# Expert-weight matrices in batches of eight tokens, built by VectorE and ScalarE alone

## The reference

```
e = (jnp.take_along_axis(i1, ci // PEER_TOPK, axis=-1) * N_KEYS
     + jnp.take_along_axis(i2, ci % PEER_TOPK, axis=-1))
g = jax.nn.softmax(sc.astype(jnp.float32), axis=-1).astype(h.dtype)
...
act = jnp.einsum('td,tkd->tk', xt, u_tab[et])
return jnp.einsum('tk,tkd->td', jax.nn.gelu(act, approximate=False) * gt, v_tab[et])
```

## Time and profile before

| | us |
|---|---|
| median of three runs | 1732.82 (1732.2 to 1737.53) |
| profiled execution | 1729.81 |
| its span, first to last instruction | 1728.0 |
| PE busy in it | 1652.7 (96%) |
| DVE busy | 1554.6 (90%) |
| ACT busy | 865.5 (50%) |
| POOL busy | 652.7 (38%) |

### The profile page before, as it was taken

One profiled execution on the slowest core, in us unless ns is written; L12 is line 12 of the kernel. 1 busy time (PEld: TensorE's weight loads), 2 busy tenths in 40 slices (PEclk: granted clock), 3 DMA queues, 4 the chain that ended last, 5 costly groups with the idle time before them and its releaser, 6 DMA issues.

```text
span 1728.0 us, 29685 instructions
## 1 busy us (share of the span) xinstructions
PE 1652.7 (96%) x9219; PEld 1387.0 (80%) x9219; DVE 1554.6 (90%) x3206; ACT 865.5 (50%) x2431; POOL 652.7 (38%) x644
## 2 busy tenths in 40 slices
PE   6999889999947999999999999999999999999997
PEld 4566658866636888889999998999999999999996
DVE  3887864499999999999999999999999999999998
ACT  3122573337788994444444444444444444444444
POOL 0000000044458983444444444344444444443442
PEclk9999999999978999999999999999999999999999
DMA  9343102111136779999999999999999999999996
GB/s 359 135 146 112 72 4 97 63 60 51 49 122 208 209 222 356 400 393 402 410 398 395 409 397 396 407 405 398 403 406 394 407 407 394 395 412 406 401 401 211
DMA packets 129315, 505.90 MB, mean 293 GB/s; under 512 B 9184, under 2 KB 64096, under 8 KB 79968
## 3 DMA queue, kind: packets, MB, share of 16 engines
q0 software_dynamic: 36864, 268.45, 38.5%
q1 hardware_dynamic: 92096, 236.49, 36.8%
q10 hardware_dynamic: 288, 0.13, 0.0%
HBM read 477.18 MB, written 25.10 MB: 291 GB/s over the span
## 4 chain that ended last, share of the span: by engine, by line
PE 78%; DVE 15%; issue 3%; ACT 2%; DMA 1%; POOL 0%; SPq 0%; DVEq 0%; POOLq 0%; ACTq 0%
PE psum L851 30%; PE psum L865 30%; PE psum L501 7%; DVE slab L1700 5%; PE psum L739 3%; DVE slab L1704 2%; PE psum L502 2%; DVE slab L1555 1%; DMA slab<-wblk 1%; PE psum L489 1%; DVE slab L1557 1%; PE psum L754 1%; DVE slab L1571 1%; ACT slab L1099 1%; DVE slab L1550 1%
## 5 line engine op out<-in xcount | busy, mean ns | idle before, releaser
L1881 POOL DMA_INDIRECT slab<-table,ixr x256 | 421.0, 1644 | 603.1 <-DVE slab L1750 552.1
L851 PE MATMUL psum<-hhi,uhi 128*128 128x384 f32 x1008 | 339.0, 336 | 1.4 <-issue 1.3
L851 PE MATMUL psum<-hhi,ulo 128*128 128x384 f32 x1008 | 338.4, 336 | 0.0
L851 PE MATMUL psum<-hlo,uhi 128*128 128x384 f32 x1008 | 337.7, 335 | 0.0
L1750 DVE SCALAR_TENSOR_TENSOR slab<-slab,cf 128x1024 f32<-128x1024 f32 x252 | 323.2, 1283 | 14.5
L1740 DVE SCALAR_TENSOR_TENSOR slab<-slab,h2tok 128x1024 f32<-128x1024 f32 x256 | 312.1, 1219 | 25.7 <-DMA slab<-table,ixr 25.4
L865 PE MATMUL psum<-vhi,whi 128*128 128x512 f32 x762 | 297.8, 391 | 3.1 <-DVE wlo L1723 3.1
L865 PE MATMUL psum<-vhi,wlo 128*128 128x512 f32 x762 | 300.1, 394 | 0.0
L865 PE MATMUL psum<-vlo,whi 128*128 128x512 f32 x762 | 299.8, 393 | 0.0
L501 PE MATMUL psum<-slab 128*128 128x512 f32 x464 | 239.1, 597 | 1.9 <-ACT slab L1021 1.1
L1206 ACT CAST whi<-slab 128x384 fp32r<-128x384 f32 x127 | 65.3, 515 | 304.3 <-DVE slab L1735 304.3
(11 more groups left out here) (240 smaller groups left out, 2771.7 us busy)
## 6 DMA issues: line engine op xcount, KB each, us to landing
slab<-ublk SPq DMA_DIRECT2D x64, 1024.0 KB, 9.0
slab<-vtab SPq DMA_DIRECT2D x63, 1024.0 KB, 8.9
slab<-wblk SPq DMA_DIRECT2D x90, 512.0 KB, 4.5
g_dram<-slab SPq DMA_DIRECT2D x11, 1984.0 KB, 8.8
slab<-g_dram SPq DMA_DIRECT2D x31, 704.0 KB, 8.9
slab<-table,ixr POOLq DMA_INDIRECT x256, 10.0
slab<-slab SPq DMA_DIRECT2D x42, 64.0 KB, 10.9
x<-x_in SPq DMA_DIRECT2D x1, 2560.0 KB, 9.2
```

What stands on the lines that cost most here:

```text
L851: last = pe.matmul(psum[:, b, 0:ND], w[:, c, :], m[:, c, :], start=(m_ == 0), stop=(m_ == 3 * DC - 1))
L1881: pool.indirect_dma_start(out=rows[:, sl % GR, :], out_offset=None, in_=table, in_offset=bass.IndirectOffsetOnAxis(ap=ixr[:, half, half_co ...
```

## The change

G is built in batches of eight tokens (`BATCH`, 48 batches), and POOL takes no part. For a batch DVE compares the second halves of eight tokens with 0 to 127 in one bf16 tensor_tensor into `same`, which has the token as its innermost index (L1691 in the new kernel). The table `iota8`, each number eight times, is made once, ahead of the search; `e2b` holds the second halves in bf16. A second tensor_tensor writes all eight rows of `hot_a` (L1695). A third multiplies four tokens of `same` by their weights and writes four rows of `hot_b` through a transposed view (L1698). ACT writes the other four rows of `hot_b` by four scaled copies out of `same`, each reading one token, that is every eighth bf16 (L1152). There are two buffers of `same`, `hot_a` and `hot_b`, eight tokens each. PE does the same matmuls as before; the first four of a batch wait for `hot_a` and ACT's rows, the second four for DVE's rows; in steps 0, 1 and 3 it also waits until ACT has read the bank's earlier contents. POOL issues its first four row fetches together.

```
@@ -141,7 +141,9 @@
-FETCH_AT = (2, 3, 4, 5)
+BATCH = 8
+NB = ND // BATCH
+OWN = BATCH // 2
...
@@ -205,7 +207,9 @@
-        e1T, e2T, gT = (sb(n, [P, ND]) for n in ("e1T", "e2T", "gT"))
+        iota8 = sb("iota8", [P, KEYS, BATCH], BF16)
+        e2b = sb("e2b", [P, ND], BF16)
+        e1T, gT = (sb(n, [P, ND]) for n in ("e1T", "gT"))
...
@@ -262,9 +266,9 @@
-        gnT, away = view(38016, ND), view(256, 4, KEYS)
+        same = [view(c0, KEYS * BATCH // 2).bitcast(BF16).rearrange("p (k t) -> p k t", t=BATCH) for c0 in (256, 37248)]
...
-        hot_a, hot_b = view(9216, 4, 4, P), view(3072, 4, 4, P)
+        hot_a, hot_b = view(9216, 2, BATCH, P), view(3072, 2, BATCH, P)
...
@@ -326,15 +330,9 @@
-        def token_of(b):
-
-            return g_group(b * 4 // TG) * TG + b * 4 % TG
-
-        def hot_a_split(b):
-
-            if b in FETCH_AT:
-                return 0
-            return 1 if b % 4 == 3 else 2
+        def first_token(n):
+
+            return g_group(n * BATCH // TG) * TG + n * BATCH % TG
...
@@ -821,13 +819,18 @@
-                pe.wait_ge(hot_a_set, sum(hot_a_split(n) > 0 for n in range(b + 1)))
-                pe.wait_ge(hot_b_set, b + 1)
-                pe.wait_ge(hot_c_set, b + 1)
+                at, half = divmod(b, 2)
+                if half:
+                    pe.wait_ge(hot_d_set, at + 1)
+                else:
+                    pe.wait_ge(hot_a_set, at + 1)
+                    pe.wait_ge(hot_c_set, at + 1)
                 if b >= 4:
                     pe.wait_ge(g_laid, b - 3)
+                elif b + 4 in SLOT_BANK:
+                    pe.wait_ge(slot_set, SLOT_BANK.index(b + 4) + 1)
                 for m in range(4):
-                    last = pe.matmul(psum[:, 4 + b % 4, m * P:(m + 1) * P], hot_a[:, b % 4, m, :], hot_b[:, b % 4, m, :], start=True, stop=True)
+                    last = pe.matmul(psum[:, 4 + b % 4, m * P:(m + 1) * P], hot_a[:, at % 2, 4 * half + m, :], hot_b[:, at % 2, 4 * half + m, :], start=True, stop=True)
...
@@ -1137,24 +1140,17 @@
-                act.copy(gT[:, t * P:(t + 1) * P], psum[:, SLOT_BANK[k], P:2 * P])
-                act.activation(gnT[:, t * P:(t + 1) * P], psum[:, SLOT_BANK[k], P:2 * P], ACT.Copy, scale=-1.0).then_inc(slot_set, 1)
-
-            def distance(b):
...
-                act.activation(away[:, b % 4, :], con[:, C_IOTA:C_IOTA + KEYS], ACT.Abs, bias=e2T[:, col:col + 1], scale=-1.0).then_inc(away_set, 1)
-
-            def hot_row(b):
...
-                act.activation(hot_b[:, b % 4, 3, :], away[:, b % 4, :], ACT.Relu, bias=gT[:, col:col + 1], scale=gnT[:, col:col + 1])\
-                    .then_inc(hot_c_set, 1)
+                act.copy(gT[:, t * P:(t + 1) * P], psum[:, SLOT_BANK[k], P:2 * P]).then_inc(slot_set, 1)
+
+            def hot_rows(n):
+
+                col, b = first_token(n), n % 2
+                act.wait_ge(same_set, n + 1)
+                if n >= 2:
+                    act.wait_ge(g_made, 2 * n - 2)
+                for m in range(OWN):
+                    last = act.activation(hot_b[:, b, m, :], same[b][:, :, m], ACT.Copy, scale=gT[:, col + m:col + m + 1])
+                last.then_inc(hot_c_set, 1)
...
@@ -1169,15 +1165,11 @@
-            for b in range(3):
-                distance(b)
-            for b in range(2):
-                hot_row(b)
+            hot_rows(0)
             for b in range(ND // 4):
-                if b + 3 < ND // 4:
-                    distance(b + 3)
-                if b + 2 < ND // 4:
-                    hot_row(b + 2)
+                at, half = divmod(b, 2)
+                if not half and at + 1 < NB:
+                    hot_rows(at + 1)
...
@@ -1617,6 +1609,7 @@
+            step(v.tensor_copy(iota8[:], con[:, C_IOTA:C_IOTA + KEYS].unsqueeze(2).broadcast_to([P, KEYS, BATCH])))
             v.tensor_copy(count, con[:, C_AT:C_AT + CAND].unsqueeze(2).broadcast_to([P, CAND, EARLY])).then_inc(topk_step, 1)
...
-                step(v.tensor_copy(e2T[:, part], e2u[:]))
+                step(v.tensor_copy(e2b[:, part], e2u[:]))
...
@@ -1690,30 +1683,35 @@
+            def hot_batch(n):
+                col, b = first_token(n), n % 2
+                if n >= 2:
+                    v.wait_ge(hot_c_set, n - 1)
+                    v.wait_ge(hot_d_set, n - 1)
+                v.tensor_tensor(same[b], iota8[:], e2b[:, col:col + BATCH].unsqueeze(1).broadcast_to([P, KEYS, BATCH]), ALU.is_equal).then_inc(same_set, 1)
+                if n >= 2:
+                    v.wait_ge(g_made, 2 * n - 2)
+                wide = [P, BATCH, KEYS]
+                v.tensor_tensor(hot_a[:, b], con[:, C_IOTA:C_IOTA + KEYS].unsqueeze(1).broadcast_to(wide),
+                                e1T[:, col:col + BATCH].unsqueeze(2).broadcast_to(wide), ALU.is_equal).then_inc(hot_a_set, 1)
+                v.wait_ge(same_set, n + 1)
+                v.tensor_tensor(hot_b[:, b, OWN:].rearrange("p t k -> p k t"), same[b][:, :, OWN:],
+                                gT[:, col + OWN:col + BATCH].unsqueeze(1).broadcast_to([P, KEYS, BATCH - OWN]), ALU.mult).then_inc(hot_d_set, 1)
+
             for k in range(N_DENSE):
                 v.wait_ge(slot_set, k + 1)
-                for b in range(k * P // 4, (k + 1) * P // 4):
-                    if b >= 4:
-                        v.wait_ge(g_made, b - 3)
-                    for m in range(3):
-                        col = token_of(b) + m
-                        v.tensor_scalar(hot_b[:, b % 4, m, :], con[:, C_IOTA:C_IOTA + KEYS], e2T[:, col:col + 1], gT[:, col:col + 1],
-                                        ALU.is_equal, ALU.mult)
-                    m0 = hot_a_split(b)
-                    col, wide = token_of(b) + m0, [P, 4 - m0, KEYS]
-                    v.tensor_tensor(hot_a[:, b % 4, m0:4, :], con[:, C_IOTA:C_IOTA + KEYS].unsqueeze(1).broadcast_to(wide),
-                                    e1T[:, col:col + 4 - m0].unsqueeze(2).broadcast_to(wide), ALU.is_equal).then_inc(hot_b_set, 1)
-                    within = b % (P // 4)
+                for n in range(k * P // BATCH, (k + 1) * P // BATCH):
+                    hot_batch(n)
+                    within = n % (P // BATCH)
...
-                    if k == 0 and within == 0:
+                    if n == 0:
                         late_sums()
-                    elif k == 0 and within == 1:
                         row_numbers()
...
@@ -1898,22 +1896,11 @@
-            for k in range(N_DENSE):
-                pool.wait_ge(halves_set, k + 1)
-                for b in range(k * P // 4, (k + 1) * P // 4):
...
-                    for m in range(hot_a_split(b)):
-                        last = pool.tensor_scalar(hot_a[:, b % 4, m, :], con[:, C_IOTA:C_IOTA + KEYS], e1T[:, col + m:col + m + 1], None, ALU.is_equal)
-                    last.then_inc(hot_a_set, 1)
+            pool.wait_ge(row_numbers_set, 1)
+            pool.tensor_copy(ixr[:, 0, :], idxf[:, 0:8]).then_inc(ix_copied, 1)
+            pool.wait_ge(ix_copied, 1)
+            for sl in range(GR):
+                fetch_row(sl, 0, sl)
```

More of the change, by code:

```diff
@@ L303, in build @@
         paced_pool = sem("paced_pool"); by_slot = sem("by_slot"); slot_number = sem("slot_number"); slot_set = sem("slot_set"); tried = sem("tried"); dense_looked = sem("dense_looked"); halves_set = sem("halves_set"); row_numbers_set = sem("row_numbers_set")
-        hot_a_set = sem("hot_a_set"); hot_b_set = sem("hot_b_set"); hot_c_set = sem("hot_c_set"); away_set = sem("away_set")
+        hot_a_set = sem("hot_a_set"); hot_c_set = sem("hot_c_set"); hot_d_set = sem("hot_d_set"); same_set = sem("same_set");
         g_made = sem("g_made"); v_first = sem("v_first"); w_first = sem("w_first"); whi_first = sem("whi_first"); wlo_first = sem("wlo_first"); quad_in = [sem("quad_in0"), sem("quad_in1")]; g_laid = sem("g_laid"); hsplit = sem("hsplit"); uhi_set = sem("uhi_set"); ulo_set = sem("ulo_set")
@@ L1707, in _ @@
                     if k + 1 < N_DENSE:
-                        if within == 18:
+                        if within == 9:
                             split_number(k + 1)
-                        elif within == 20:
+                        elif within == 10:
                             number_halves(k + 1)
-                        elif within == 22:
+                        elif within == 11:
                             halves_ready()
-                    if k == 0 and within == 0:
+                    if n == 0:
@@ L1900, in _ @@
             pool.wait_ge(h2_tok, 2 * N_GATHER)
-            for k in range(N_DENSE):
-                pool.wait_ge(halves_set, k + 1)
-                for b in range(k * P // 4, (k + 1) * P // 4):
-                    if b >= 4:
-                        pool.wait_ge(g_made, b - 3)
-                    if b == FETCH_AT[0]:
-                        pool.wait_ge(row_numbers_set, 1)
-                        pool.tensor_copy(ixr[:, 0, :], idxf[:, 0:8]).then_inc(ix_copied, 1)
-                        pool.wait_ge(ix_copied, 1)
```

(9 more changed lines are left out.)

6 lines of the change are left out of this document (removed).

## The result

The kernel after the change takes 1741.98 us (median; 1738.53 to 1744.91), the kernel before, run beside it, 1733.13 us. The ratio is 1.0045, with a 95% interval of 1.0035 to 1.0054: slower by some 8 us, where the prediction had 17. The direction holds, and the range of 1740 to 1764 us holds at its lower end, which had been drawn for the rival in which only ACT pays; the size is off by a factor of two.

A forecast was written before the change was run, and what follows sets the result against it. DVE's instruction stream was taken to bound G: 2.80 us a batch against 2.47, over 48 batches 16 us more, plus 1 at the end, 17 in all. Forecast 1750 us on the median's scale, range 1740 to 1764.

The forecast's parts named there:

- only ACT pays: Rival for G: hops cost ACT but not DVE, DVE 2.33 and ACT 2.64 a batch, 9 us slower, 1742; chance 0.07.
- What bounds G, and that what DVE loses there moves the end: DVE's instruction stream bounds G; PE's loop follows untouched, so DVE's gain or loss before 648 us moves the end equally.
- The bf16 compare at 0.60 and the f32 compare at 1.13: DVE's first two instructions per batch in G, each over 1024 elements: 0.60 us and 1.13 us from start to start.
- The multiply at 1.07: DVE's third instruction per batch, 512 elements: 0.60 us plus 0.47 for write hops, priced from L1637's read hop of 0.91 ns.
- The sentence on the Trainium skill: Rule that DVE keeps its rate only in runs of two adjacent words; 1.71 ns an element hopping 4 KiB, 2.50 stepping 24 words.
- ACT at 0.42 a copy, 2.64 a batch, with 0.16 us of cover: ACT in G: 0.96 plus four hopping copies of 0.42 makes 2.64 us, under DVE's 2.80, so ACT costs nothing.
- the end, forecast at 1 us: End of G: ACT's last copies come later relative to DVE, whose weights need them; 1 us more.
- Hops free: Rival for G: hops cost neither engine, multiply 0.60, DVE 2.33 a batch, kernel 1727 us; chance 0.20.
- ACT above 0.46: Rival for G: a scaled copy above 0.46 us makes ACT the bound; at 0.50 the kernel takes 1758 us; chance 0.10.
- dearer write hop: Rival for G: a write hop costs more than a read hop, multiply 1.30 to 1.54, kernel 1761 to 1772; chance 0.08.
- PE, the clock, DMA, the table of keys: PE at most 2.32 us a batch, clock unchanged, no DMA wait, table instruction under 0.9 us hidden in DVE's 1.36 wait.
- POOL's removal buys nothing by itself: In G all POOL comparisons vanish; having no row in the chain of waits, this gains nothing by itself.

The follow-up runs named there:

- e1: Kernel after the change, with DVE's multiply writing its 512 results in one run instead of 512 bytes apart; 1742.73 us, ratio to the kernel before 1.0045.
- m1: Kernel after the change, with groups of four equal instructions, eight forms on DVE and eight on ACT, appended to read single prices; time not compared.
- e2: Kernel after the change, with ACT's four scaled copies reading 128 neighbouring values instead of every eighth; 1741.52 us, ratio to the kernel before 1.0045.
- e8: Kernel before the change, with GpSimd's compares left out from the ninth step of four tokens on; 1730.94 us, ratio to the unedited kernel before 0.9987.

## Why the prediction was right, and where it was wrong

*What bounds G, and that what DVE loses there moves the end:* held in part. G grew by 7.7, the tail by 1.5, the time by 8.85; the loop did not change. But DVE is no longer the only bound: ACT stands level with it.

*The bf16 compare at 0.60 and the f32 compare at 1.13:* held, 0.60 and 1.12.

*The multiply at 1.07:* **this is the step that failed.** It takes 0.90. The mechanism was right (with the hop gone it takes 0.60, as e1 shows), the size of the hop was taken from the wrong row. L1637's 0.91 ns is for a reduction that reads 32 B apart; a tensor_tensor pays 0.75 for reading at that step, 0.68 for reading 512 B apart and 0.60 for writing 512 B apart (m1). So roughly half of the error came from the operation, the rest from the step and the direction. The difference, 0.17 x 48 = 8.2 us, is the whole gap between 17 and the 8.85 measured. The sentence on the Trainium skill, which the sum did not use, was nearer: by the 1.71 ns of Vector Engine (DVE) Microarchitecture Reference, section 5.2, the multiply was estimated at 0.95 and the kernel at 11 us more. The trace agrees to within 6%: 0.90 in the kernel, 0.91 in m1, which is 1.78 ns an element with all that an instruction costs in it. No run here hopped by the 4 KiB of that figure, or stepped by the 24 words of the other.

*ACT at 0.42 a copy, 2.64 a batch, with 0.16 us of cover:* the price held (0.42 and 2.62), with some luck: it took a hop to cost the same at any step, and at 8 B, half the step, the copy would have cost 0.305 (m1). The cover did not exist, since it was the distance to the mis-sized 2.80. At 2.62 ACT is level with DVE. That has two effects. The hops of neither engine are worth removing alone (e1, e2). And the end, forecast at 1 us, came out at 1.5, because ACT enters the tail without slack; with slack the wait disappears (e2).

*Only ACT pays, 1742 us*, the rival with a chance of 0.07, has the measured time, but only half of its mechanism: it had DVE at 2.33, and DVE is at 2.62. Yet e1, which puts DVE at 2.33, has the same time, so ACT alone would have been enough. For every multiply from 0.60 to 0.90 ACT's 2.64 gives the same 1742 (measured at both ends, worked out between them). This stretch is a third of the bounds that the prediction had set (0.60 to 1.54), and the chance of 0.07 took only their end at 0.60. That the range holds is owed to this rival and not to the multiply of 1.07. *Hops free* and *ACT above 0.46* fell with the prices, the *dearer write hop* with m1: at the same 512 B a write costs 0.91, a read 0.95.

*PE, the clock, DMA, the table of keys:* held. The granted clock stays at 1.00 with PE at 35.74 of 47 us. DVE's wait for PE in the search, shrank from 1.36 to 0.76 and covered the new instruction:

```profile
352.83 0.68 DVE L1612 CAST iota<-con 128x1024 bf16<-128x1024 f32 x1
...
360.74 0.49 DVE L1542 MAX8 slab<-psum 128x8 f32<-128x128 f32 x2 [0.76 <-PE psum L777]
```

*POOL's removal buys nothing by itself:* the reason given was incomplete. It had no row in the chain, but it lengthened the rows of DVE that were there, by 0.17 us for eight tokens (e8). The sum is not harmed, because the new instructions were priced from rows that agree with an idle POOL; but the true cost of the change's layout is then against DVE work of 2.30 for eight tokens, not 2.47, of which PE and ACT let G have only 4.9 us in all.

## What to carry to other kernels

Price a strided access from a row with the same operation, the same direction, read or write, and the same step, or measure it; a reduction's read hop of 32 B was half as dear again as a tensor_tensor's write hop of 512 B. When a change gives two engines equal work per batch, undoing either half shows nothing, so test both together, and before trusting a cover ask how large it is if the other term was overpriced. Where one layout must serve a wide compare and narrow readers, pairs of 2-byte elements, which put each reader's step at 4 B, cost neither side anything here.
